# Stick-breaking attention on one Trainium2 core: two passes over V with its high and low parts in one stationary tile, and a bank for each head

## The chip, the cores and the metric

The kernel runs on one core of a Trainium2 chip. A core has five engines with queues of their own: TensorE (matrix products, into the eight PSUM banks of 128 x 512 float32), VectorE, ScalarE, GpSimd, and SyncE, which issues DMAs. Engines work in order, each through its own queue, and meet only at semaphores. The metric is device time in microseconds for one call. `PE`, `PEld`, `DVE`, `ACT`, `POOL` and `SP` in the profile are TensorE's products, TensorE's weight loads, VectorE, ScalarE, GpSimd and SyncE.

## The reference

One sequence of 512 tokens, width 1024, two layers: a stick-breaking attention layer (16 heads of 64), then a differential attention layer on a shared K and V. Only the first layer is touched. Cut to it:

```python
def stick_breaking_attention(q, k, v):          # (B,H,S,D), strictly causal
    z = einsum('bhqd,bhkd->bhqk', q, k) / sqrt(D)
    log_1m = where(strict, log_sigmoid(-z), 0.0)
    suffix = cumsum(log_1m, axis=3, reverse=True) - log_1m
    a = where(strict, exp(log_sigmoid(z) + suffix), 0.0)
    return einsum('bhqk,bhkd->bhqd', a, v)

def stick_breaking_layer(x, norm_g, w_in, w_out):
    h = rms_norm(x, norm_g)
    q, k, v, gate = split(h @ w_in, 4)           # each (S, 1024), heads of 64
    o = stick_breaking_attention(heads(q), heads(k), heads(v))
    return (silu(gate) * o) @ w_out
```

Everything is float32, and the kernel gets float32 accuracy out of products on rounded operands (float32r) by splitting: each operand is a high part (rounded) and a low part (the rest), and a product is hi·hi + hi·lo + lo·hi, three passes of TensorE.

## The kernel before

Each of the five engines has one hand-written program (`@block.tensor`, `@block.vector`, `@block.scalar`, `@block.gpsimd`, `@block.sync`), and what one engine needs of another is a `wait_ge` on a named semaphore. The order inside an engine is therefore the order of the code.

**Stages.** Norm and transpose of the input, the projection of V for all heads (to 78 us of the profile), then eight *pairs* of heads (p = 0 to 7, 128 features each, 78 to 311 us), the first output projection (to about 350 us), then the second layer, which the change does not touch. Pair 0 and pair 7 are written out, pairs 1 to 6 are a loop. Weights come in slabs of 128 x 512 by DMA; GpSimd splits each into `w_hi` (a cast, L468) and `w_lo` (a subtraction, L470).

**A pair on TensorE** (`pair`, L692 to L717). `scores_a(p)` waits for q and k to be split (`s_qk`, L646), puts masks into banks 0 to 5 (L637, L639) and adds the scores (L658), head h in banks 3h to 3h+2. `attend_a(p-1, 1)` then finishes the *previous* pair in bank 7. Then the gate's projection into bank 6, and the projection of the next q into bank 7 in two halves of 12 matmuls of 512 columns, with `suffix_sums(p, 0)` between them; `suffix_sums(p, 1)`; the projection of the next k into bank 6; `attend_a(p, 0)` into bank 7. A projection is 24 matmuls of 512 columns (L560, L561, L562, the lines of `three`). The next pair starts with its scores.

The scores of a head are kept transposed as four causal strips, j = 0 to 3, 512, 384, 256 and 128 columns wide (`STRIP`), 1280 columns in all. `attend_a(p, h)` multiplies each strip of weights (`hi[h]`, `lo[h]`) with the 128 x 128 stationary tile of V for that strip. V lies as `va_hi` and `va_lo`, 192 columns per strip: head 0 at 0 to 63, zeros at 64 to 127, head 1 at 128 to 191. Columns 0 to 127 are thus head 0 beside zeros, columns 64 to 191 zeros beside head 1, and both heads can add into one bank, head 0 in rows 0 to 63 and head 1 in rows 64 to 127:

```python
                v = slice(DH * h, DH * h + P)
                mm = three(o[:, j * P:SEQ], va_hi[:, j, v], va_lo[:, j, v], hi[h][:, seg], lo[h][:, seg],
                           start=(h == 0 and j == 0), stop=(h == 1 and j == TT - 1))
```

**A pair on ScalarE** (L1057 to L1109). For each of the six score banks an abs (`ab`, L1062), an exp (`e`, L1067) and a log (`l`, L1072), interleaved; the gate's copy, abs, exp and log; `weights(h)`: the exponentials of the suffix sums (L1078, L1080); between and after them `q_hi_a` (L1004) and, last in the pair, `k_hi_a` (L1009), the high parts of the next q and k, which wait for their projections.

**A pair on VectorE** (L1374 to L1428). For each score bank `soft` (softplus, L1378, one input in PSUM), `soft_hi` (a cast, L1384) and `soft_lo` (a subtraction, L1389, both inputs in SBUF); `suffix_sums(p, 0)` waits for the three soft_lo of head 0, `suffix_sums(p, 1)` for those of head 1. Behind the first soft_lo stands `gated_a(p-1)` (L1372): the previous pair's output in bank 7 times `silu`. It frees bank 7 (`s_og`, L710) and feeds `keep_hi` and `keep_lo`, the split output that the output projection reads. Then the gate's part, `weights_lo(h)` (L1395), `q_lo_a` (L1324) and, last, `k_lo_a` (L1330).

**GpSimd** splits V for a pair (`values_a`, L482 and L484) once `attend_a(p-1, 1)` is done (`s_pv`), then that pair's slabs.

**Pair 7** has no next q and k. In their place `early_tile` multiplies six kept outputs with the first six slabs of the output weights; `attend_a(7, 1)` runs after the sixth step of the output projection and step k = 7 waits for the last kept output (`s_o`).

## Time and profile before

| | us |
|---|---|
| median of three runs | 695.98 (693.69 to 698.03) |
| the profiled execution, its own time | 692.85 |
| its span, first to last instruction | 691.6 |
| TensorE busy | 646.1 |
| VectorE / ScalarE / GpSimd busy | 433.1 / 328.6 / 343.8 |

The profile is one execution. Its page gives shares of the span; the windows give the same for a stretch, with the clock that TensorE was granted (1.00 is 2.4 GHz, 0.50 is 1.2 GHz); the timeline gives start and length of each instruction, and in brackets how long the engine sat idle before it and what ended that. Matmuls overlap: one's length is longer than the distance to the next, and the distance between two starts is what it costs. The same holds in part for VectorE and ScalarE, whose next instruction can start before the last one's end.

### The profile page before, as it was taken

What the parts mean: (1) busy time and instruction counts of PE and PEld (TensorE: products, weight loads), DVE (VectorE), ACT (ScalarE), POOL (GpSimd) and SP (SyncE); (2) the same over time, 40 slices, a digit from 0 to 9 for tenths busy, and PEclk for the clock granted to TensorE, in tenths of its full rate; (3) what the DMA queues carried; (4) which work ended last, traced back from release to release, by engine and by line L of the source; (5) the groups of instructions that cost most, each with busy time, mean ns of one, the idle gap of its engine ahead of it and who ended that gap; (6) DMA issues with size and microseconds to landing.
All of it is one profiled execution on the core that took longest, in us unless ns stands there. A gap on an engine that the chain in (4) does not pass through costs nothing.

```text
span 691.6 us, 10026 instructions
## 1 busy us (share of the span) xinstructions
PE 646.1 (93%) x3388; PEld 544.9 (79%) x3388; DVE 433.1 (63%) x685; ACT 328.6 (48%) x712; POOL 343.8 (50%) x325
## 2 busy tenths in 40 slices
PE   4999989999999999899989999997899889687998
PEld 4788778888888888788878888886787777576886
DVE  3493295775957758473073788048888899777321
ACT  4342466475664756633255454224564356535220
POOL 5564675544555442445324544485744465253241
PEclk9999999999999999999999999999999999878999
DMA  7432231221212210021112222223222111210141
GB/s 243 119 91 77 67 102 46 62 61 45 61 45 61 61 45 30 16 77 62 65 58 88 95 85 83 84 76 99 78 65 57 34 42 46 87 51 26 50 138 61
DMA packets 61774, 49.08 MB, mean 71 GB/s; under 512 B 7729, under 2 KB 48817, under 8 KB 61745
## 3 DMA queue, kind: packets, MB, share of 16 engines
q1 hardware_dynamic: 58064, 48.25, 22.6%
q10 hardware_dynamic: 3680, 0.46, 0.4%
q8 instruction: 17, 0.28, 0.2%
q14 instruction: 13, 0.10, 0.0%
HBM read 44.50 MB, written 2.10 MB: 67 GB/s over the span
## 4 chain that ended last, share of the span: by engine, by line
PE 72%; DVE 16%; issue 5%; ACT 3%; POOL 2%; DMA 1%; DVEq 0%; SPq 0%; POOLq 0%; ACTq 0%
PE bank L560 19%; PE bank L561 19%; PE bank L562 19%; PE bank L673 6%; DVE small L1585 3%; PE bank L658 2%; DVE ge L1340 1%; DVE pr L1608 1%; PE bank L821 1%; POOL w_lo L470 1%; PE bank L841 1%; DVE v L1308 1%; DVE hi L1384 1%; DMA xs<-in_x 1%; PE bank L637 1%
## 5 line engine op out<-in xcount | busy, mean ns | idle before, releaser
L470 POOL TENSOR_TENSOR w_lo<-w_raw,w_hi 128x512 fp32r<-128x512 f32 x100 | 139.6, 1396 | 8.0
L458 POOL TENSOR_TENSOR w_lo<-w_raw,w_hi 128x512 fp32r<-128x512 f32 x60 | 81.1, 1354 | 122.0 <-ACT w_hi L954 121.6
L468 POOL CAST w_hi<-w_raw 128x512 fp32r<-128x512 f32 x100 | 72.3, 723 | 123.1 <-PE bank L562 74.2
L560 PE MATMUL bank<-h_hi,w_hi 128*128 128x512 f32 x320 | 130.8, 409 | 2.6 <-ACT q L1152 2.6
L560 PE MATMUL bank<-w_hi,h_hi 128*128 128x512 f32 x320 | 127.6, 399 | 4.0 <-DVE h_lo L1314 2.9
L561 PE MATMUL bank<-h_lo,w_hi 128*128 128x512 f32 x320 | 127.1, 397 | 0.0
L562 PE MATMUL bank<-h_hi,w_lo 128*128 128x512 f32 x320 | 126.7, 396 | 0.0
L562 PE MATMUL bank<-w_hi,h_lo 128*128 128x512 f32 x320 | 125.2, 391 | 0.0
L561 PE MATMUL bank<-w_lo,h_hi 128*128 128x512 f32 x320 | 125.1, 391 | 0.0
L560 PEld LDWEIGHTS bank<-h_hi,w_hi 128*128 128x128 f32 x320 | 61.8, 193 | 15.9 <-ACT q L1152 3.0
L954 ACT ACTIVATE w_hi<-w_raw 128x512 fp32r<-128x512 f32 x60 | 37.6, 628 | 77.0 <-PE bank L562 77.0
L560 PEld LDWEIGHTS bank<-w_hi,h_hi 128*128 128x128 f32 x320 | 60.5, 189 | 16.9 <-DVE h_lo L1314 3.5
L562 PEld LDWEIGHTS bank<-h_hi,w_lo 128*128 128x128 f32 x320 | 61.2, 191 | 13.8
L561 PEld LDWEIGHTS bank<-h_lo,w_hi 128*128 128x128 f32 x320 | 61.5, 192 | 11.7
L562 PEld LDWEIGHTS bank<-w_hi,h_lo 128*128 128x128 f32 x320 | 60.2, 188 | 13.2
L561 PEld LDWEIGHTS bank<-w_lo,h_hi 128*128 128x128 f32 x320 | 60.4, 189 | 12.0
L1378 DVE SCALAR_TENSOR_TENSOR sp<-bank,ex 128x512 f32<-128x512 f32 (+1 forms) x48 | 28.4, 593 | 42.8 <-ACT ex L1072 42.8
L1234 ACT ACTIVATE pr<-bank,small 128x512 f32<-128x512 f32 (+3 forms) x64 | 38.8, 616 | 11.8 <-DVE small L1590 11.8
L1389 DVE TENSOR_TENSOR lo<-sp,hi 128x512 fp32r<-128x512 f32 (+1 forms) x48 | 42.6, 888 | 0.6
L1496 DVE TENSOR_TENSOR xs<-bank,xs 128x512 f32<-128x512 f32 x16 | 10.9, 692 | 46.1 <-PE bank L562 46.1
L1395 DVE TENSOR_TENSOR lo<-ex,hi 128x512 fp32r<-128x512 f32 (+1 forms) x48 | 33.5, 752 | 7.4 <-ACT hi L1080 7.4
L1062 ACT ACTIVATE ex<-bank 128x512 f32<-128x512 f32 (+1 forms) x48 | 25.3, 527 | 24.1 <-PE bank L658 23.4
(176 smaller groups left out, 1229.7 us busy)
## 6 DMA issues: line engine op xcount, KB each, us to landing
w_raw<-in_a_w_in SPq DMA_DIRECT2D x64, 256.0 KB, 2.8
w_raw<-in_w_kv SPq DMA_DIRECT2D x32, 256.0 KB, 3.1
w_raw<-in_b_w_in SPq DMA_DIRECT2D x32, 256.0 KB, 2.8
w_raw<-in_a_w_out SPq DMA_DIRECT2D x16, 256.0 KB, 2.7
w_raw<-in_b_w_out SPq DMA_DIRECT2D x16, 256.0 KB, 2.8
xs<-in_x SPq DMA_DIRECT2D x4, 512.0 KB, 5.3
qrot<-qs SPq DMA_DIRECT2D x32, 64.0 KB, 2.0
out_x<-xs SPq DMA_DIRECT2D x8, 256.0 KB, 2.6
```

Of the source, the lines that this page charges most:

```text
L458: nc.gpsimd.tensor_tensor(w_lo[s][:, :], w_raw[s][:, :], w_hi[s][:, :].bitcast(F32), ALU.subtract).then_inc(s_w, 1)
L468: nc.gpsimd.tensor_copy(w_hi[s][:, :], w_raw[s][:, :]).then_inc(s_whi, 1)
L470: nc.gpsimd.tensor_tensor(w_lo[s][:, :], w_raw[s][:, :], w_hi[s][:, :].bitcast(F32), ALU.subtract).then_inc(s_w, 1)
L560: pe.matmul(o, ahi, bhi, start=start, stop=False, skip_group_check=True)
L561: pe.matmul(o, ahi, blo, start=False, stop=False, skip_group_check=True)
L562: return pe.matmul(o, alo, bhi, start=False, stop=stop, skip_group_check=True)
L673: mm = pe.matmul(bank[3 * h + b][:, cols(c, n)], (neg_tri if i == j else neg_one)[:, :], part[h][:, cols(STRIP[i][0], n)], start=False, st ...
L954: A(w_hi[s][:, :], w_raw[s][:, :], ACT.Copy).then_inc(s_whia, 1)
L1234: A(pr[c][:, cols(at, w)], bank[BANK_B[c, b]][:, cols(at - BANKS[b][0], w)], ACT.Exp, bias=tiny[:, 8 + 2 * i + c:9 + 2 * i + c], scale=mea ...
L1378: STT(out=sp[m // 3][:, seg], in0=bank[m][:, 0:BANKS[m % 3][1]], scalar=0.0, op0=ALU.max, in1=ex[m // 3][:, seg], op1=ALU.add).then_inc(s_ ...
L1389: TTN(lo[h][:, seg], sp[h][:, seg], hi[h][:, seg].bitcast(F32), ALU.subtract).then_inc(s_sl, 1)
L1395: TTN(lo[h][:, seg], ex[h][:, seg], hi[h][:, seg].bitcast(F32), ALU.subtract).then_inc(s_al, 1)
```

## The change

V is laid out anew. One tile `va` holds, for each strip and head, 128 stationary columns: the high part of V's 64 columns and its low part side by side, for head 0 high then low, for head 1 low then high. One pass with `hi[h]` and one with `lo[h]` then give, in 64 rows of the bank, the weights times V's high part (rows of that head) and, in the other 64, the weights times V's low part, which contains the lo·lo product too. The two halves must be added, across partitions: ScalarE copies the low half to the head's own rows in SBUF (`correction` into `cor`), VectorE adds (`sum_output` into `osum`), and `gated_a` takes `osum` in place of the bank. Since a head now fills a whole bank, head 0 goes into bank 0 (free once its weights are made) and head 1 into bank 7 (bank 3 in pair 7). `attend_a(p, 0)` moves from behind the key projection to between its halves, and the wait for q_lo ahead of it goes. The scores wait for head 0's sum (bank 0), the projection of q waits for head 1's (bank 7). On ScalarE head 1's correction stands between `l(1)` and `ab(3)` of the next pair, head 0's behind `weights(1)`; on VectorE head 1's sum takes the place that `gated_a` had, which moves behind `soft_hi(1)`, and head 0's stands behind `weights_lo(1)`. GpSimd splits V with four instructions per pair in place of two, and the two memsets of the old tiles go. In pair 7 head 1's correction stands behind the slab G_OUT + 11 on ScalarE.

```diff
--- before.py
+++ after.py
@@ -198,8 +198,9 @@
     w_raw += [sb(f"w_raw{i}", [P, 512], F32, phase_a) for i in (4, 5)]
     w_hi += [sb(f"w_hi{i}", [P, 512], F32R, phase_a) for i in (4, 5)]
     w_lo += [sb(f"w_lo{i}", [P, 512], F32R, phase_a) for i in (4, 5)]
-    va_hi = sb("va_hi", [P, TT, 192], F32R, phase_a)
-    va_lo = sb("va_lo", [P, TT, 192], F32R, phase_a)
+    va = sb("va", [P, TT, 2, P], F32R, phase_a)
+    cor = sb("cor", [P, SEQ], F32, phase_a)
+    osum = sb("osum", [P, SEQ], F32, phase_a)
     ex = [sb(f"ex{h}", [P, CAUSAL], F32, phase_a) for h in (0, 1)]
     sp = [sb(f"sp{h}", [P, CAUSAL], F32, phase_a) for h in (0, 1)]
     hi = [sb(f"hi{h}", [P, CAUSAL], F32R, phase_a) for h in (0, 1)]
@@ -268,6 +269,9 @@
     s_al = sem("weights_split")
     s_v = sem("v_split")
     s_pv = sem("block_output_ready")
+    s_pa = sem("first_output_ready")
+    s_cor = sem("correction_copied")
+    s_os = sem("output_summed")
     s_gc = sem("gate_copied")
     s_ga = sem("gate_abs")
     s_gx = sem("gate_exp")
@@ -313,7 +317,7 @@
     wout_b = b_w_out.rearrange("o (k p) n -> p (o k) n", p=P)
     x_rows = x.rearrange("o (t p) n -> p (o t) n", p=P)
     out_rows = out.rearrange("o (t p) n -> p (o t) n", p=P)
-    va_parts = [v[:, :, :].rearrange("p j (a b) -> p j a b", a=3)[:, :, 0:3:2, :] for v in (va_hi, va_lo)]
+    va_parts = [[va[:, :, h, cols(DH * (h ^ part), DH)] for h in (0, 1)] for part in (0, 1)]
     ang = ex[0][:, 0:640]
     turns, absr = ex[1][:, 0:640], sp[1][:, 640:1280]
     sines = sp[0]
@@ -440,11 +444,10 @@
         nc.gpsimd.affine_select(out=g32[:, 2 * P:3 * P], in_=big, compare_op=ALU.is_gt, fill=0.0, base=0,
                                 pattern=[[1, P]], channel_multiplier=-1)
         nc.gpsimd.memset(ones_c, 1.0)
-        nc.gpsimd.memset(va_hi[:, :, :].bitcast(F32), 0.0)
         st.link(nc.gpsimd.memset(sel, 0.0))
         st.link(nc.gpsimd.memset(sel[0:DH, 0:1], 1.0))
-        st.link(nc.gpsimd.memset(sel[DH:P, 1:2], 1.0))
-        nc.gpsimd.memset(va_lo[:, :, :].bitcast(F32), 0.0).then_inc(s_cst, 1)
+        nc.gpsimd.memset(sel[DH:P, 1:2], 1.0).then_inc(s_cst, 1)
+        pool.wait_ge(s_cst, 1)
 
         def waited():
 
@@ -472,9 +475,19 @@
 
         def values_a(p):
 
-            src = v32[:, :, bass.ds(p * P, P)].rearrange("p j (a b) -> p j a b", a=2)
             pool.wait_ge(s_pv, p)
-            split_v(src, va_parts[0], va_parts[1])
+            split_pair([v32[:, :, bass.ds(p * P + DH * h, DH)] for h in (0, 1)])
+
+        def split_pair(src):
+
+            waited()
+            for h in (0, 1):
+                ins = nc.gpsimd.tensor_copy(va_parts[0][h], src[h])
+            st.link(ins)
+            waited()
+            for h in (0, 1):
+                ins = nc.gpsimd.tensor_tensor(va_parts[1][h], src[h], va_parts[0][h].bitcast(F32), ALU.subtract)
+            ins.then_inc(s_v, 1)
 
         def split_v(src, dhi, dlo):
 
@@ -488,7 +501,7 @@
         pool.wait_ge(s_vk, V_BY_ACT)
         pool.wait_ge(s_vkd, 2)
 
-        split_v(v32[:, :, 0:P].rearrange("p j (a b) -> p j a b", a=2), va_parts[0], va_parts[1])
+        split_pair([v32[:, :, cols(DH * h, DH)] for h in (0, 1)])
         for g in range(G_BODY + 2, G_BODY + 12):
             split(g)
         with pool.Fori(1, KT - 2) as i:
@@ -646,6 +659,7 @@
             pe.wait_ge(s_qk, p * 2 + 2)
             if not first:
                 pe.wait_ge(s_ah, p * 6)
+                pe.wait_ge(s_os, p * 2 - 1)
             for h in (0, 1):
                 for b in range(3):
                     mask(bank[3 * h + b][:, :], 0, len(BANK_STRIPS[b]), 3 * P, mask_a)
@@ -675,19 +689,19 @@
                                            skip_group_check=True)
                 mm.then_inc(s_t, 1)
 
-        def attend_a(p, h, o=bank[7]):
+        def attend_a(p, h, o=None):
 
 
             if h == 0:
                 pe.wait_ge(s_v, p + 1)
             pe.wait_ge(s_al, p * 6 + (3 * h + 3))
+            o = o or bank[7 if h else 0]
             for j in range(TT):
-                v = slice(DH * h, DH * h + P)
                 seg = cols(*STRIP[j])
-                mm = three(o[:, j * P:SEQ], va_hi[:, j, v], va_lo[:, j, v], hi[h][:, seg], lo[h][:, seg],
-                           start=(h == 0 and j == 0), stop=(h == 1 and j == TT - 1))
-            if h == 1:
-                mm.then_inc(s_pv, 1)
+                for w in (hi, lo):
+                    mm = pe.matmul(o[:, j * P:SEQ], va[:, j, h, :], w[h][:, seg], start=(j == 0 and w is hi),
+                                   stop=(j == TT - 1 and w is lo), skip_group_check=True)
+            mm.then_inc(s_pv if h else s_pa, 1)
 
         def pair(p, first=False, last=False):
 
@@ -698,23 +712,21 @@
             project(G_GLAST if last else G_BODY, h1_hi, h1_lo, bank[6][:, :], p, 0 if last else 6)
             if last:
                 suffix_sums(p, 0)
-                pe.wait_ge(s_og, p)
+                pe.wait_ge(s_os, p * 2)
                 early_tile(0)
                 pe.wait_ge(s_gc, p + 1)
                 pe.wait_ge(s_ga, p + 1)
                 early_tile(1)
                 suffix_sums(p, 1)
-                attend_a(p, 0, bank[0])
+                attend_a(p, 0)
                 return
             if not first:
-                pe.wait_ge(s_og, p)
+                pe.wait_ge(s_os, p * 2)
             project(G_BODY + 2, h1_hi, h1_lo, bank[7][:, :], p, 6, between=lambda: suffix_sums(p, 0))
             suffix_sums(p, 1)
             pe.wait_ge(s_gc, p + 1)
             pe.wait_ge(s_ga, p + 1)
-            project(G_BODY + 4, h1_hi, h1_lo, bank[6][:, :], p, 6)
-            pe.wait_ge(s_qk, p * 2 + 3)
-            attend_a(p, 0)
+            project(G_BODY + 4, h1_hi, h1_lo, bank[6][:, :], p, 6, between=lambda: attend_a(p, 0))
 
         def early_tile(t):
 
@@ -734,7 +746,7 @@
         pair(KT - 1, last=True)
         for k in range(EARLY):
             bulk_step(G_OUT + k, 0, k, h2_hi, h2_lo, banks_of=OUT_BANK_A, tiles=(2, 3))
-        attend_a(KT - 1, 1, bank[0])
+        attend_a(KT - 1, 1, bank[3])
         for k in range(EARLY, KT):
             pe.wait_ge(s_o, k + 1)
             bulk_step(G_OUT + k, 0, k, h2_hi, h2_lo, banks_of=OUT_BANK_A)
@@ -1087,6 +1099,8 @@
             l(0)
             e(2)
             l(1)
+            if not first:
+                correction(p - 1, 1, bank[7])
             ab(3)
             l(2)
             ab(4)
@@ -1105,8 +1119,17 @@
             if not last:
                 q_hi_a(p * 6 + (G_BODY + 4))
             weights(1)
+            correction(p, 0, bank[0], first)
             if not last:
                 k_hi_a(p * 6 + (G_BODY + 6))
+
+        def correction(p, h, o, first=False):
+
+            act.wait_ge(s_pv if h else s_pa, p + 1)
+            if not first:
+                act.wait_ge(s_os, p * 2 + (h - 1))
+            main, other = slice(DH * h, DH * h + DH), slice(DH - DH * h, P - DH * h)
+            A(cor[main, :], o[other, :], ACT.Copy).then_inc(s_cor, 1)
 
         pair(0, first=True)
         with act.Fori(1, KT - 1) as i:
@@ -1114,7 +1137,10 @@
         pair(KT - 1, last=True)
 
 
-        for g in range(G_OUT + RING_A, G_OUT + 14):
+        for g in range(G_OUT + RING_A, G_OUT + 12):
+            slab_hi(g)
+        correction(KT - 1, 1, bank[3])
+        for g in range(G_OUT + 12, G_OUT + 14):
             slab_hi(g)
         for t in range(TT):
             squares(1, t, 0)
@@ -1366,10 +1392,16 @@
             keep_hi(p, n)
             keep_lo(p, n)
 
-        def gated_a(p, o=bank[7]):
-
-            dve.wait_ge(s_pv, p + 1)
-            TTN(og[:, :], o[:, :], silu[:, :], ALU.mult).then_inc(s_og, 1)
+        def sum_output(p, h, o):
+
+            main = slice(DH * h, DH * h + DH)
+            dve.wait_ge(s_cor, p * 2 + (h + 1))
+            TTN(osum[main, :], o[main, :], cor[main, :], ALU.add).then_inc(s_os, 1)
+
+        def gated_a(p):
+
+            dve.wait_ge(s_os, p * 2 + 2)
+            TTN(og[:, :], osum[:, :], silu[:, :], ALU.mult).then_inc(s_og, 1)
 
         def pair(p, first=False, last=False):
             def soft(m):
@@ -1399,8 +1431,10 @@
             soft(1)
             soft_lo(0)
             if not first:
+                sum_output(p - 1, 1, bank[7])
+            soft_hi(1)
+            if not first:
                 gated_a(p - 1)
-            soft_hi(1)
             soft(2)
             soft_lo(1)
             soft_hi(2)
@@ -1424,6 +1458,7 @@
             if not last:
                 q_lo_a(p * 2 + 3)
             weights_lo(1)
+            sum_output(p, 0, bank[0])
             if not last:
                 k_lo_a(p * 2 + 4)
 
@@ -1485,7 +1520,8 @@
             pair(i)
             st.leave(KT - 2)
         pair(KT - 1, last=True)
-        gated_a(KT - 1, bank[0])
+        sum_output(KT - 1, 1, bank[3])
+        gated_a(KT - 1)
         keep_output(KT - 1, KT)
 
         def add_residual(g, m, half, banks_of=range(8)):
```

## Rows read from the trace of the kernel before

**Rows 1.** The page, busy time of each engine (share of the span), instructions
```profile
PE 646.1 (93%) x3388; PEld 544.9 (79%) x3388; DVE 433.1 (63%) x685; ACT 328.6 (48%) x712; POOL 343.8 (50%) x325
```

**Rows 2.** Windows: length, busy us (instructions) per engine, PEclk (granted clock), DMA, GB/s
```profile
166.00:195.00 29.00, 29.00 (x170) 25.19 (x169) 20.35 (x31) 17.63 (x37) 14.87 (x15) 1.00 0.19 54
...
199.60:212.95 13.35, 13.35 (x67) 11.29 (x67) 13.20 (x22) 10.13 (x22) 8.07 (x8) 1.00 0.20 59
```

**Rows 3.** Timeline of TensorE, a hand-over: start, length (start us, us), line, form, count
```profile
192.72 0.39 PE L560 MATMUL bank<-hi,va_hi 128*128 128x512 f32 x1
...
194.57 0.28 PE L637 MATMUL bank<-mask_a,ident_r 128*128 128x128 f32 x1
...
197.46 0.50 PE L560 MATMUL bank<-hi,va_hi 128*128 128x512 f32 x1
...
199.43 0.45 PE L560 MATMUL bank<-h_hi,w_hi 128*128 128x512 f32 x1
...
223.40 0.28 PE L637 MATMUL bank<-mask_a,ident_r 128*128 128x128 f32 x1
```

**Rows 4.** Timeline of TensorE, the suffix sums of the same pair
```profile
207.81 0.40 PE L673 MATMUL bank<-hi,neg_tri 128*128 128x512 f32 x1
...
209.03 0.39 PE L673 MATMUL bank<-hi,neg_tri 128*128 128x384 f32 x1
...
213.31 0.40 PE L673 MATMUL bank<-hi,neg_tri 128*128 128x512 f32 x1
```

**Rows 5.** Timelines of ScalarE (first row) and VectorE in the same pair
```profile
192.91 0.60 ACT L1009 ACTIVATE k_hi<-bank 128x512 fp32r<-128x512 f32 x1 [3.84 <-PE bank L562]
...
193.55 0.69 DVE L1330 TENSOR_TENSOR k_lo<-bank,k_hi 128x512 fp32r<-128x512 f32 x1 [2.83 <-ACT k_hi L1009]
...
201.28 1.22 DVE L1389 TENSOR_TENSOR lo<-sp,hi 128x512 fp32r<-128x512 f32 x1
...
203.43 0.41 DVE L1378 SCALAR_TENSOR_TENSOR sp<-bank,ex 128x256 f32<-128x256 f32 x1
...
208.01 0.68 DVE L1378 SCALAR_TENSOR_TENSOR sp<-bank,ex 128x512 f32<-128x512 f32 x1
...
208.61 0.69 DVE L1389 TENSOR_TENSOR lo<-sp,hi 128x512 fp32r<-128x512 f32 x1
...
212.50 0.43 DVE L1389 TENSOR_TENSOR lo<-sp,hi 128x256 fp32r<-128x256 f32 x1
```

**Rows 6.** Timelines of ScalarE and GpSimd in the same pair
```profile
200.77 0.42 ACT L1072 ACTIVATE ex<-ex 128x256 f32<-128x256 f32 x1
...
200.66 1.29 POOL L484 TENSOR_TENSOR va_lo<-v,va_hi 128x512 fp32r<-128x512 f32 x1 [0.19 <-POOL va_hi L482]
```

**Rows 7.** VectorE's groups, shapes apart, six looped pairs: busy us, mean ns, idle before
```profile
L1389 DVE TENSOR_TENSOR lo<-sp,hi 128x512 fp32r<-128x512 f32 x24 | 24.2, 1007 | 0.0
...
L1372 DVE TENSOR_TENSOR og<-bank,silu 128x512 f32<-128x512 f32 x6 | 4.1, 678 | 0.0
```

**Rows 8.** Timelines of TensorE and VectorE, pair 7 and the output projection
```profile
302.92 0.50 PE L560 MATMUL bank<-w_hi,h_hi 128*128 128x512 f32 x1 [1.05 <-POOL w_lo L470]
...
324.07 0.69 DVE L1362 TENSOR_TENSOR h_lo<-og,h_hi 128x512 fp32r<-128x512 f32 x1
...
325.47 0.39 PE L560 MATMUL bank<-w_hi,h_hi 128*128 128x512 f32 x1
```

**Rows 9.** Windows of pair 7, columns as in the second group
```profile
291.70:293.78 2.08, 0.05 (x1) 0.00 (x0) 2.05 (x3) 1.93 (x4) 2.00 (x3) 1.00 0.34 126
...
295.44:298.85 3.41, 3.41 (x15) 3.22 (x14) 3.41 (x5) 2.08 (x5) 3.25 (x5) 0.50 0.27 95
```

**Rows 10.** Timelines of TensorE in pair 0 and of GpSimd at the start
```profile
97.88 0.50 PE L673 MATMUL bank<-hi,neg_tri 128*128 128x512 f32 x1 [1.34 <-DVE lo L1389]
...
2.79 0.74 POOL L443 MEMSET va_hi<- 128x768 f32 x1
```

## The prediction

> **What bounds the kernel now.** I read the page's engine shares first: TensorE is busy 93% of the span [rows 1]. An average does not say what a change in one stage is worth, so next I took the windows of the stick-breaking stage: in a stretch as long as one looped head pair TensorE is busy for 29.00 of 29.00 us at the full clock, GpSimd for half of it [rows 2]. The masks of two pairs start at 194.57 and 223.40, so a pair takes 28.83 us [rows 3]. In this stage matmul time is the time, as long as nothing that TensorE waits for comes later. The last view, the timelines of one pair, tells how far each such thing is from coming later, and that decides this change.
>
> Three slacks matter. (1) After the key projection, k_hi (ScalarE) and k_lo (VectorE) must be made before the next pair's scores. The first slot after the projection is at 192.72; k_lo ends at 193.55 + 0.69 = 194.24; the masks start at 194.57 [rows 3, 5]. The wait is hidden by `attend_a(p, 0)`, which fills 192.72 to 194.57. (2) `suffix_sums(p, 1)` starts at 213.31 and needs the last soft_lo, which ends at 212.50 + 0.43 = 212.93: 0.38 us of room, or 0.34 after the 0.04 that a release takes (k_hi ends at 192.91 + 0.60 = 193.51, k_lo starts at 193.55) [rows 4, 5]. (3) From 199.60 to 212.95 VectorE is busy for 13.20 of 13.35 us [rows 2]: what is added there moves its end.
>
> **The change, part by part.**
>
> *The third pass goes.* Each head has 4 strips x 3 matmuls, 1.85 us (192.72 to 194.57) for head 0 and 1.97 (197.46 to 199.43) for head 1 [rows 3]. After it, 4 strips x 2. The first eight matmuls of the suffix sums have just these widths, two each of 512, 384, 256 and 128: 207.81 to 209.03 = 1.22 us [rows 4]. That is 0.63 less per head, 16 x 0.63 = 10.1 us of matmul time in all.
>
> *Head 0 moves between the halves of the key projection.* It keeps its cost, now 1.22, but no longer covers the copies of k: those end at 194.24, released 0.04 later, against the slot at 192.72, a wait of 1.56 us. From projection to masks it was 1.85; now it is 1.22 + 1.56 = 2.78. That is +0.93 at seven hand-overs (pair 0 to 1, up to 6 to 7): **+6.5 us**.
>
> *ScalarE's correction of head 0 and VectorE's sum* stand ahead of k_hi and k_lo in their queues. A matmul of 512 takes 0.233 (199.43 to 207.81 is 36 of them [rows 3, 4]), so head 0 ends 12 x 0.233 = 2.8 us ahead of the projection's end; correction (as k_hi, 0.60) and sum (as k_lo, 0.69) are over more than 1 us before it. No cost; without that cover k_hi would be late by what is missing. The scores' new wait on this sum costs nothing either: k_lo comes later in the same queue.
>
> *Head 1's correction on ScalarE, ahead of `ab(3)`.* Head 1 starts at 197.46 and now ends near 198.8. `l(2)` runs at 200.77, one slot behind `ab(3)` [rows 6], so ScalarE comes to the correction near 200.3, does not wait, and loses about 0.5 us. Queued behind it are l(2) and head 1's softplus. l(2) then ends near 201.7, and soft(2), which needs it, starts at 203.43 [rows 5]; those behind have more. Hidden.
>
> *VectorE's front.* `sum_output(p-1, 1)` is one more instruction on PSUM, 0.60 us of queue time (208.01 to 208.61 [rows 5]). Beside it `gated_a` changes kind: its input was a bank, now both inputs are in SBUF. The bank form took 678 ns in the loop; soft_lo of the same size with both inputs in SBUF took 1007 on average [rows 7], though 0.69 at best. At 201.28 it took 1.22 and ended soon after a GpSimd instruction did (200.66 + 1.29 = 201.95) [rows 5, 6]. So I add 0.33 and get e = 0.93. Lower bound 0.60 (the gating meets no GpSimd work), upper 0.60 + 1.3 = 1.9 (it waits for a whole GpSimd subtraction). In this stretch GpSimd is busy 8.07 of 13.35 us, so meeting it is likelier than not. TensorE comes 0.63 earlier, VectorE 0.93 later, 0.34 is room: a wait of 1.2 us, and suffix_sums(p, 1) starts 0.59 later after the scores than before. Pair 0 has neither sum nor gating ahead of it and pair 7 waits elsewhere, so six pairs: **+3.5 us**, between the bounds +1.6 and +9.4. Head 1's own 0.63 is swallowed here.
>
> That the two-input form waits behind GpSimd is what these rows show. The Trainium skill (SBUF — State Buffer, "Who interferes with whom") has it as a rule: a VectorE instruction with two SBUF inputs contends with a GpSimd instruction that reads SBUF, and one with at most one, outside the two-port modes, does not. By that rule the gating leaves the safe kind; had it stayed, this term would be 6 x 0.26 = 1.6 us.
>
> *Pair 7 and the end.* GpSimd splits v after head 1 of pair 6, then six slabs, and TensorE waits for the sixth until 302.92 [rows 8]. The splitting starts 0.63 earlier, but does four instructions instead of two; and half an instruction costs more than half its time: 0.19 us pass even between the two now [rows 6], I estimate 0.15 for each of the two added, 0.3 in all: -0.3. A later VectorE chain is covered by this wait. Head 0: -0.63. Head 1: -0.63, but output step k = 7 needs the gated output, there at 324.07 + 0.69 = 324.76 against its slot at 325.47, room 0.71 [rows 8]. Correction and sum put 0.60 + 0.69 + 0.08 = 1.37 into that chain: +0.66. Net 0. Together **-0.9 us**.
>
> *GpSimd's split of v in the loop*: four instructions of half the size on an engine busy half the time. Nothing. *The start*: two memsets of 0.74 leave [rows 10] and the warm-up matmuls start 1.5 us earlier; the first products wait for DMA, ScalarE and VectorE. I take 0. TensorE's idle time before the transposes grows by as much; should the clock rise later for it, that could cost what one stretch at the lower clock costs (B below), 1.7.
>
> **Sum.** 6.5 + 3.5 - 0.9 = 9.1 us, slower. The profiled execution took 692.85 (span 691.6); the median of the runs, 695.98, is 3.1 above it, and waits add alike to both: 702.0 beside the profile's time, **705.1** beside the median.
>
> **Rivals.**
>
> *A: VectorE absorbs its extra work.* For it: in the loop the 24 wide soft_lo alone lose 24 x 0.32 = 7.6 us behind GpSimd, 1.3 per pair [rows 7], and GpSimd's work now starts 0.63 earlier after the scores, so these losses may shrink. Against it: the sum is certain, the shrinking is luck. With e at -0.29 or lower TensorE sets the pace, -0.63 per pair: 6.5 - 3.8 - 0.9 = +1.8, **697.8**, not slower than can be told. It decides from e = 0.57 down, where the sum falls below 7.0.
>
> *B: the clock falls after the new waits.* After some 2.03 us of idling up to 293.78 the granted clock was 0.50 from 295.44 to 298.85: 3.41 us at 1.2 instead of 2.4 GHz, 1.7 lost. After 1.34 us of idling before 97.88 it stayed at 1.00 [rows 9, 10]. The new waits, 1.6 and 1.2, lie between or below. If four of the seven hand-overs met it: +6.8, **711.9**.
>
> *C: the lock at its upper bound.* e = 1.9: 6.5 + 9.4 - 0.9 = 15.0, **711.0**.
>
> *D: no wait is exposed and the change brings its matmul time*: -10.1, **685.9**. Against it stands the order: nothing is left between the key projection and the scores, whose first instruction waits for k_lo. It needs the two copies of k to take nearly no time.
>
> **How the numbers follow.** Forecast (e from 0.57 to 1.5, no fall of the clock) 0.52; A 0.22; B 0.09; C 0.11; D 0.06. The likeliest gives 705.1; its own range is 703 to 709. The range reaches from A's 697.8 to B's 711.9, rounded outwards, and leaves out D and the far sides of B and C, under 2 in 10. One per cent is 7 us, about what a measurement of this kernel can tell from no change. Slower: B, C and all of the forecast but 0.06 that other mis-sized terms bring under 702.9: 0.66. Same: A and that 0.06: 0.28. Faster: D, 0.06.
>
> **What would show it.** Right: 64 matmuls fewer; a head's attention near 1.22 us; TensorE idle about 1.6 us before each of seven first masks, released by k_lo, and about 1.2 before suffix_sums(p, 1), released by soft_lo; a pair every 28.83 + 0.93 + 0.59 = 30.35 us; the gating above 0.68 in some pairs. Wrong: a pair in under 29.9 us (A), a granted clock of 0.50 inside the loop (B), a wait for a correction or a sum before the last pair, or masks that start without a wait (D).

## The result, and the profile after

The changed kernel takes 709.19 us (median of six runs, 706.75 to 709.92) against 697.53 for the kernel before on the same chip: ratio **1.017**, 95% interval 1.014 to 1.020, some 12 us slower. Forecast was 9.1 us slower, 705.1 in the range 697.5 to 712.5. The profiled execution took 708.09 us, 15.2 more than that of before. The medians differ by 11.7: the execution profiled before took 4.7 us less than the median of its kernel's six runs, this one 1.1 less, so 3.6 of the 15.2 are not the change's. The page after, against [rows 1]:

```profile
PE 643.1 (91%) x3324; PEld 535.8 (76%) x3324; DVE 451.3 (64%) x701; ACT 337.1 (48%) x728; POOL 347.5 (49%) x339
```

TensorE has 64 matmuls less, yet its busy time is only 3.0 us less; the 15.2 us and these 3 are idle time. The removed matmuls are 10.1 us at their pace. What makes up for most of them is that two stretches ran at the lower clock which the kernel before does not have (below, about 1.7 us each), and that at each new wait the last matmul's length, 0.39 where the next slot is 0.23 on, counts as busy and the first one behind the wait is slow. The masks of the eight pairs tell where it lies. All in us, the first matmul of each:

| | before | after | difference |
|---|---|---|---|
| start to first masks of pair 0 | 78.71 | 79.62 | +0.9 |
| first masks to suffix_sums(p, 1), pair 0 | 19.17 | 19.46 | +0.3 |
| the same, pairs 1 to 6, sum | 112.48 | 118.37 | +5.9 |
| suffix_sums(p, 1) to the next masks, seven, sum | 70.70 | 79.47 | +8.8 |
| pair 7 and output projection, to the start of its last addition | 69.28 | 69.39 | +0.1 |
| second layer | 341.2 | 340.5 | -0.7 |

**The hand-over.** Timeline of TensorE after, answering to [rows 3]: head 0 between the halves of the key projection, the projection's last matmul, the masks.

```profile
197.68 0.39 PE L702 MATMUL bank<-hi,va 128*128 128x512 f32 x1
...
198.90 0.45 PE L573 MATMUL bank<-h_hi,w_hi 128*128 128x512 f32 x1
...
201.48 0.39 PE L575 MATMUL bank<-h_hi,w_lo 128*128 128x512 f32 x1
203.45 0.32 PE L650 MATMUL bank<-mask_a,ident_r 128*128 128x128 f32 x1 [1.59 <-DVE k_lo L1356]
```

And ScalarE (first two rows) and VectorE beside it, against [rows 5]:

```profile
199.18 0.60 ACT L1132 ACTIVATE cor<-bank 64x512 f32<-64x512 f32 x1 [2.43 <-PE bank L702]
201.90 0.60 ACT L1021 ACTIVATE k_hi<-bank 128x512 fp32r<-128x512 f32 x1 [2.12 <-PE bank L575]
...
199.81 0.68 DVE L1399 TENSOR_TENSOR osum<-bank,cor 64x512 f32<-64x512 f32 x1 [0.78 <-ACT cor L1132]
202.53 0.69 DVE L1356 TENSOR_TENSOR k_lo<-bank,k_hi 128x512 fp32r<-128x512 f32 x1 [2.04 <-ACT k_hi L1021]
```

Head 0 takes 198.90 - 197.68 = 1.22 us, as forecast. Then the last matmul of the key projection starts at 201.48, the next slot would be 201.71, the masks start at 203.45, released by k_lo. Correction and sum are over (199.81 + 0.68 = 200.49) when k_hi starts: they do not hold it up. The waits of TensorE for one line each, total, number, longest, over the pairs:

```profile
PE bank L650 <- DVE k_lo L1356: 11.0, 7, 1.6
PE bank L687 <- DVE lo L1421: 5.7, 10, 1.1
```

Seven waits for k_lo, and ten for soft_lo. **The front.** The two waits for soft_lo in a pair, against [rows 4], and VectorE in the next pair, against [rows 5]:

```profile
185.87 0.50 PE L687 MATMUL bank<-hi,neg_tri 128*128 128x512 f32 x1 [0.64 <-DVE lo L1421]
...
192.06 0.50 PE L687 MATMUL bank<-hi,neg_tri 128*128 128x512 f32 x1 [0.41 <-DVE lo L1421]
```

```profile
208.56 0.69 DVE L1410 SCALAR_TENSOR_TENSOR sp<-bank,ex 128x512 f32<-128x512 f32 x1 [5.34 <-ACT ex L1084]
...
211.33 0.69 DVE L1399 TENSOR_TENSOR osum<-bank,cor 64x512 f32<-64x512 f32 x1
212.06 1.38 DVE L1416 CAST hi<-sp 128x512 fp32r<-128x512 f32 x1
213.36 0.68 DVE L1404 TENSOR_TENSOR og<-osum,silu 128x512 f32<-128x512 f32 x1
...
215.01 1.38 DVE L1416 CAST hi<-sp 128x256 fp32r<-128x256 f32 x1
...
222.62 0.42 DVE L1421 TENSOR_TENSOR lo<-sp,hi 128x256 fp32r<-128x256 f32 x1
```

GpSimd in the same stretch:

```profile
211.85 1.30 POOL L473 TENSOR_TENSOR w_lo<-w_raw,w_hi 128x512 fp32r<-128x512 f32 x1
...
214.59 1.65 POOL L473 TENSOR_TENSOR w_lo<-w_raw,w_hi 128x512 fp32r<-128x512 f32 x1
```

Two casts (soft_hi, L1416) take 1.38 us: that at 212.06 ends at 213.44, behind GpSimd's instruction of 211.85 + 1.30 = 213.15; that at 215.01 at 216.39, behind 214.59 + 1.65 = 216.24. VectorE's groups in the six looped pairs, before, beside [rows 7], and after:

```profile
L1384 DVE CAST hi<-sp 128x512 fp32r<-128x512 f32 x24 | 18.3, 762 | 0.4
...
L1389 DVE TENSOR_TENSOR lo<-sp,hi 128x256 fp32r<-128x256 f32 x12 | 7.7, 641 | 0.4
...
L1384 DVE CAST hi<-sp 128x256 fp32r<-128x256 f32 x12 | 3.4, 281 | 0.0
```

```profile
L1416 DVE CAST hi<-sp 128x512 fp32r<-128x512 f32 x24 | 21.8, 909 | 0.6
...
L1421 DVE TENSOR_TENSOR lo<-sp,hi 128x512 fp32r<-128x512 f32 x24 | 16.9, 703 | 0.0
...
L1416 DVE CAST hi<-sp 128x256 fp32r<-128x256 f32 x12 | 10.0, 834 | 0.0
...
L1421 DVE TENSOR_TENSOR lo<-sp,hi 128x256 fp32r<-128x256 f32 x12 | 5.6, 463 | 0.4
L1404 DVE TENSOR_TENSOR og<-osum,silu 128x512 f32<-128x512 f32 x6 | 5.2, 863 | 0.0
```

The cast of 512 columns has gone from 762 to 909 ns, that of 256 from 281 to 834, while soft_lo has gone from 1007 to 703 and from 641 to 463. The waits have moved to other instructions; their total has hardly changed (the four groups take 54.3 us for 53.6). The gating's mean of 863 ns hides that it took 0.68 us in five of the six pairs, as before, and this once in the sixth:

```profile
244.50 1.78 DVE L1404 TENSOR_TENSOR og<-osum,silu 128x512 f32<-128x512 f32 x1
```

**The clock.** Windows of the hand-over into pair 5 and of the stretch behind it:

```profile
232.90:234.50 1.60, 0.02 (x1) 0.00 (x0) 0.69 (x1) 0.60 (x1) 1.32 (x2) 1.00 0.44 131
236.34:239.75 3.41, 3.41 (x22) 2.99 (x19) 0.00 (x0) 2.68 (x6) 0.00 (x0) 0.50 0.26 75
```

Here, after 1.59 us of idling, the granted clock fell to 0.50. Behind the six other hand-overs, which idle for 1.41 to 1.64 us, it stayed at 1.00. The pair took 32.32 us where the three ahead of it took 31.04 to 31.08. At the start, from 21.3 to 24.7 us, it was 0.50 too, and in the kernel before it was not; the stretch in pair 7, from 311.6 on, the kernel before has as well [rows 9].

### The profile page after: what moved, and what is told of

Its sections match the earlier page's. It is cut to its first block, busy times and chain, and to the rows that moved or that the text cites. A ratio compares the mean times of both kernels' runs of the same rounds, so it can differ in the third digit from the quotient of the medians.

```text
span 706.8 us, 9976 instructions
## 1 busy us (share of the span) xinstructions
PE 643.1 (91%) x3324; PEld 535.8 (76%) x3324; DVE 451.3 (64%) x701; ACT 337.1 (48%) x728; POOL 347.5 (49%) x339
## 4 chain that ended last, share of the span: by engine, by line
PE 57%; DVE 26%; issue 9%; ACT 6%; DMA 1%; DVEq 0%; SPq 0%; ACTq 0%
PE bank L573 14%; PE bank L575 14%; PE bank L574 14%; PE bank L687 5%; DVE lo L1421 3%; DVE hi L1416 3%; DVE small L1621 3%; DVE sp L1410 2%; PE bank L672 2%; DVE pr L1644 2%; ACT ex L1079 2%; PE bank L702 2%; DVE ge L1366 1%; PE bank L833 1%; PE bank L650 1%
## 5 line engine op out<-in xcount | busy, mean ns | idle before, releaser
L1416 DVE CAST hi<-sp 128x512 fp32r<-128x512 f32 (+1 forms) x48 | 44.5, 928 | 0.8
```

What stands on the lines that cost most here:

```text
L1416: V.tensor_copy(hi[m // 3][:, seg], sp[m // 3][:, seg]).then_inc(s_sh, 1)
```

## The experiments

Each ran beside the kernel before on the same chip; ratios are to that kernel, with their 95% intervals. "Period" is the distance between the first masks of two looped pairs, "front" that from the first masks to suffix_sums(p, 1).

### The move alone

```diff
-            project(G_BODY + 4, h1_hi, h1_lo, bank[6][:, :], p, 6)
-            pe.wait_ge(s_qk, p * 2 + 3)
-            attend_a(p, 0)
+            project(G_BODY + 4, ..., between=lambda: head0(p))   # head0: the same wait and attend_a(p, 0)
```

> The kernel before with one part of the change alone: attend_a(p, 0), still three passes, moved between the halves of the key projection. My theory (the move takes away what covered the copies of k): each of seven hand-overs gains a wait of 1.74 us, the size seen in the profile after, and 0.1 for the restart, so about +12.9 us, the loop's period 30.7 us, TensorE idle about 1.6 us before each of seven first masks. Rival (the changed kernel is slower because of its added instructions, not because of the move): between 0 and +2 us, since no instruction is added.

Measured 707.17 us, ratio 1.017 (1.014 to 1.021), +12.4 us. Period 30.60, front 18.79 (18.75 before). TensorE ahead of one of the masks:

```profile
171.42 0.32 PE L637 MATMUL bank<-mask_a,ident_r 128*128 128x128 f32 x1 [1.49 <-DVE k_lo L1333]
```

One moved call, no added instruction, costs as much as the whole change. The rival falls. In the changed kernel the hand-overs cost 8.8 us, less than here, where they cost 7 x 1.7, because head 0 is 0.63 us shorter there. Here the masks start 0.13 to 0.14 us behind k_lo's end in the loop, in the changed kernel 0.23 to 0.28.

### The third pass alone, with nothing in its place

```diff
-                mm = three(o[:, j * P:SEQ], va_hi[:, j, v], va_lo[:, j, v], hi[h][:, seg], lo[h][:, seg], ...)
+                for w in (hi, lo):
+                    mm = pe.matmul(o[:, j * P:SEQ], va_hi[:, j, v], w[h][:, seg], ...)
```

> The kernel before without its third pass and with nothing in its place: the product of V's low part is left out, so this computes less. It tells what 64 matmuls fewer are worth at best in the old order. Theory 1 (matmul time is the time): 16 x 0.63 = -10.1 us. Theory 2 (mine, by the slacks): head 0's 1.22 us no longer cover the 1.75 us of the copies of k, so a hand-over gains 0.1 and not 0.63; the front gains at most the 0.34 us that VectorE leaves; pair 7 and the end give about -1.9: 7 x -0.1 - 6 x 0.34 - 1.9 = -4.6 us, with new idle time of about 0.4 us before each first mask and about 0.3 before suffix_sums(p, 1).

Measured 694.36 us, ratio 1.000 (0.998 to 1.002). Both theories fall: in this order 64 matmuls fewer are worth nothing. In five looped pairs the period is 29.42 us, *longer* than 28.83, the front 19.42 for 18.75 (pair 6, beside which GpSimd has less to do, takes 28.66). TensorE's waits in the loop, and VectorE's softplus groups in the same window as [rows 7]:

```profile
PE bank L673 <- DVE lo L1390: 4.6, 11, 0.4
```

```profile
L1385 DVE CAST hi<-sp 128x512 fp32r<-128x512 f32 x24 | 23.4, 973 | 0.4
L1390 DVE TENSOR_TENSOR lo<-sp,hi 128x512 fp32r<-128x512 f32 x24 | 20.8, 867 | 0.0
L1385 DVE CAST hi<-sp 128x256 fp32r<-128x256 f32 x12 | 10.0, 832 | 0.0
L1390 DVE TENSOR_TENSOR lo<-sp,hi 128x256 fp32r<-128x256 f32 x12 | 5.1, 425 | 0.4
```

The four groups take 59.3 us here, 53.6 before. No instruction of VectorE or GpSimd was changed, only the moment at which TensorE finishes with a slab, and with it the moment at which GpSimd starts on the next. The casts take 11.7 us more than before, soft_lo 6.0 less. So the front of the kernel before was as quick as it was because GpSimd's instructions happened to fall where they cost VectorE less; 0.6 us earlier, they fall on its casts. In pair 7 some time is gained, 1.2 us, although about 6.8 us ran at a granted clock of 0.50 there, twice what the kernel before meets, which costs up to 1.7 us of the gain. The same kernel once more, to exclude that it is one execution's chance:

> A second look at the kernel before without its third pass (the product of V's low part is left out). Theory: the loop's period is 29.4 us again, longer than with the third pass, with two waits of about 0.4 us for soft_lo, since it is not chance but the order of GpSimd's and VectorE's instructions. Rival (one execution's chance): a period between 28.2 and 28.8.

Measured: period 29.40 to 29.44 in the same five pairs, front 19.41 to 19.43, the two waits again, casts 975 and 831 ns, 695.35 us in its one run beside a median of 693.84. Not chance.

### A shorter front for VectorE

In the changed kernel, `gated_a(p - 1)`, `keep_hi(p - 1, p)` and `keep_lo(p - 1, p)` are taken out of the softplus front and stand behind `gate_log(p + 1)`.

> The changed kernel with gated_a, keep_hi and keep_lo of the pair before moved on VectorE from the softplus front to behind gate_log; the sum of head 1 stays in the front. Theory (VectorE's front sets the start of the suffix sums): 1.65 us leave a front that is late by 1.06 in all, TensorE sets the pace again, the start of suffix_sums(p, 1) after the first mask goes from 19.65 to about 18.2 us, the period from 31.05 to 29.6, in all about -9 us against the changed kernel (700). Rival (ScalarE's correction ahead of ab(3) or GpSimd's four instructions hold the front): no more than -2.

Measured 704.88 us, ratio 1.015 (1.011 to 1.020). The front went from 19.65 to between 18.81 and 18.88, the period from 31.05 to between 29.92 and 30.17, in the pairs at the full clock; two pairs met the lower clock (30.96 and 31.68 us), which in the changed kernel's profile one had. TensorE's waits:

```profile
PE bank L650 <- DVE k_lo L1356: 9.4, 6, 1.6
PE bank L687 <- DVE lo L1421: 2.1, 5, 0.4
```

The direction of the theory holds, its size does not: of 1.65 us taken out of VectorE's queue 0.8 arrive, and a wait of 0.43 before suffix_sums(p, 0) is left of 0.65. In total the run cannot be told from the changed kernel's ratio.

### Head 0 back behind the key projection

```diff
-            project(G_BODY + 4, ..., between=lambda: attend_a(p, 0))
+            project(G_BODY + 4, ...)
+            pe.wait_ge(s_qk, p * 2 + 3)
+            attend_a(p, 0, bank[7])
```

`correction(p, 0)` and `sum_output(p, 0)` follow k_hi and k_lo, and `attend_a(p - 1, 1)` waits for that sum.

> The changed kernel with head 0 back behind the key projection, in bank 7, and its correction and sum behind k_hi and k_lo; head 1 waits for that sum. Theory (the copies of k are the hand-over's cost): the wait before the first mask falls from 1.59 us to about 0.4, a hand-over costs 1.3 us less, 7 x -1.3 = -9 us against the changed kernel (700), period 29.7 us. Rival (a head that fills a bank needs a wait somewhere: head 1's new wait for the sum takes its place): less than -3, with TensorE idle before attend_a(p-1, 1), released by the sum.

Measured 698.93 us, ratio 1.007 (1.004 to 1.010), by the ratios 1.0% or 7 us less than the changed kernel. Period 29.44 to 29.66 in pairs 1 to 5, front 19.54 to 19.64, as in the changed kernel. The waits:

```profile
PE bank L686 <- DVE lo L1423: 5.9, 10, 1.1
PE bank L650 <- DVE k_lo L1358: 1.6, 6, 0.3
```

The wait before the masks is 0.3 instead of 1.6, and none stands before head 1: the rival falls. What is left to the kernel before is the front.

### GpSimd's split of V later

In the loop `values_a` moves from ahead of the six slabs to behind the fourth, in pair 7 behind the six slabs of the output weights; once in the kernel before, once in the changed kernel.

> The kernel before with GpSimd's split of V moved, in each looped pair, from ahead of the slabs to behind the fourth slab, and in pair 7 behind the six slabs of the output weights. Theory (TensorE alone sets the loop's pace in the kernel before, VectorE's waits behind GpSimd are hidden there): period 28.8 us as it was; the gain is only in pair 7, whose slabs come earlier (idle 2.03 and 1.05 us there): -2 to -3 us. Rival (VectorE's waits do not come from GpSimd's instructions): the softplus instructions soft_hi and soft_lo of 128x512, 762 and 1007 ns on average in the loop, stay as long.

Measured 688.69 us, ratio 0.992 (0.989 to 0.994), -5.8 us. The period is 28.83 in all six pairs. From pair 7's masks to the start of the output projection's last addition it took 64.8 us for 69.3: the idle 2.03 is 0.49, the wait of 1.05 for the sixth slab is gone, and the granted clock, which fell to 0.50 there before, stays at 1.00, which is another 1.7. The rival about the instructions holds in part: soft_hi of 512 is now at 964, soft_lo at 700, and the four softplus groups take 55.0 us for 53.6. With the split of V moved away the waits did not become fewer, they only changed place, so most of them lie behind the slabs' instructions.

> The changed kernel with GpSimd's split of V moved behind the fourth slab (in pair 7 behind the six). Theory (the front is late because VectorE waits behind GpSimd): the waits for soft_lo, 0.65 and 0.41 us per pair, go, the period falls from 31.05 to about 30.0, pair 7 loses most of its 4.63 us of idling: -9 us against the changed kernel (700). Rival (VectorE's added sum and gating alone make the front late): the front stays within 0.3 us of 19.65, only pair 7 gains, -2 to -3.

Measured 709.36 us, ratio 1.021 (1.016 to 1.026). The theory falls, and the front stays within 0.3 us of 19.65, as the rival had it. In four pairs it is 19.40 to 19.42 and the period 31.2, and pair 7 with the output projection takes 68.1 us for 69.4; the two other pairs met the lower clock (32.1 and 31.9). The waits for soft_lo and a new one, for V itself:

```profile
PE bank L690 <- DVE lo L1424: 3.3, 8, 0.4
PE bank L705 <- POOL va L489: 2.5, 6, 0.9
```

### All three moves

> The changed kernel with all three moves: head 0 behind the key projection in bank 7, gating and keeping out of VectorE's front, GpSimd's split of V behind the fourth slab. Theory: TensorE sets the pace again with two passes, the period is 28.83 - 0.63 - 0.1 = 28.1 us or a little over, pair 7 gains 2 to 3 us as the kernel before would: about -8 us against the kernel before (688). Rival (two passes cannot pay in this order, since whatever TensorE gains in the front brings GpSimd's slabs, and with them VectorE's waits, forward): a period of 28.8 or more, 693 to 697.

Measured 707.37 us, ratio 1.017 (1.012 to 1.022). The front is right at last (18.58 in pair 1, with no wait of note for soft_lo), but k_lo comes late. VectorE, TensorE, and the window that follows:

```profile
166.82 4.07 DVE L1432 TENSOR_TENSOR lo<-ex,hi 128x512 fp32r<-128x512 f32 x3
170.81 0.68 DVE L1361 TENSOR_TENSOR k_lo<-bank,k_hi 128x512 fp32r<-128x512 f32 x1
...
171.62 0.47 PE L653 MATMUL bank<-mask_a,ident_r 128*128 128x128 f32 x1 [2.48 <-DVE k_lo L1361]
...
171.62:178.40 6.78, 6.78 (x34) 5.95 (x35) 0.47 (x1) 2.72 (x6) 0.00 (x0) 0.50 0.13 39
```

`weights_lo(1)`, three instructions, takes 4.07 us where it takes 2.03 in the changed kernel's loop and 1.63 in pair 0. The last two slabs, which GpSimd now splits behind V, lie beside it, and TensorE idles 2.48 us. After each of the six waits (2.38 to 2.48 us) the granted clock fell to 0.50, for up to 6.8 us, and periods behind them were 31.7 to 33.3. This is the forecast's rival B, in a kernel that was not the forecast's.

### soft_hi computed from the bank

```diff
-                V.tensor_copy(hi[m // 3][:, seg], sp[m // 3][:, seg])
+                STT(out=hi[m // 3][:, seg], in0=bank[m][:, 0:BANKS[m % 3][1]], scalar=0.0, op0=ALU.max,
+                    in1=ex[m // 3][:, seg], op1=ALU.add)
```

> The changed kernel with one kind of instruction exchanged: soft_hi is no longer a cast of sp (SBUF to SBUF) but the softplus computed once more from the bank, rounded on writing (one input in PSUM, one in SBUF). Uncontended it is longer by 0.27 us (512 columns) and 0.13 (256). Theory (the front is late because VectorE's SBUF-only instructions wait for whole GpSimd instructions): the casts lose 3.4 us per pair to those waits now, so in spite of the longer form the front is over 1 us or more sooner, the waits for soft_lo (0.65 and 0.41) go, period 31.05 to about 29.9, pair 7 gains 2: about -8 us against the changed kernel (701). Rival (VectorE's front is late by the number and length of its instructions): +1.26 us per pair, period 32.3, +7 us (716).

Measured 705.70 us, ratio 1.015 (1.009 to 1.021). Both fall in the loop: a period of 31.2 in four pairs and 29.42 in one (30.8 in the sixth, at the lower clock for a stretch). The new form never waits, but gating and keeping now do:

```profile
L1415 DVE SCALAR_TENSOR_TENSOR hi<-bank,ex 128x512 fp32r<-128x512 f32 x24 | 16.4, 681 | 0.2
...
L1404 DVE TENSOR_TENSOR og<-osum,silu 128x512 f32<-128x512 f32 x6 | 7.0, 1162 | 0.0
...
L1382 DVE CAST h_hi<-og 128x512 f32 x6 | 5.9, 980 | 0.0
```

The gating took 1.03 or 1.04 us in five pairs and 1.80 in one. In the pair of 29.42 us the front took 18.13, TensorE's own time; in the four others 19.83, with a wait of 1.11 before suffix_sums(p, 1). The gating of the kernel before, one input in PSUM, took 678 ns. In pair 0, which has no gating and no keeping in its front and where VectorE sets the pace, the exchange gave what was hoped: 28.15 for 30.89.

### What these point to

The next takes, on top of the changed kernel, head 0 behind the key projection, the shorter front, and the later split of V in pair 7 alone:

> The changed kernel with head 0 behind the key projection in bank 7, gating and keeping out of VectorE's front, and, in pair 7 alone, GpSimd's split of V behind the six slabs. Theory: the hand-over as in the run with head 0 behind the projection, the front as in the run with the shorter front: period 29.65 - 0.77 = 28.9 us, that of the kernel before, and pair 7's gain of 5 us: 689, equal to the kernel before with the same edit in pair 7, so two passes bring nothing. Rival (k_lo comes late, as in the run with all moves in the loop, because gating and keeping now stand ahead of it): period over 30, with idle time above 0.5 us before the first mask.

Measured 692.97 us, ratio 0.999 (0.996 to 1.001). Period 29.04 for the 28.9 expected, wait before the masks 0.57: the rival's mechanism is there, small. The total is 4 us over the expectation, three of them in pair 7 and the output projection, which take 67.8 us where the kernel before with the later split of V took 64.8. They have an idle 2.84 us there for 0.49, and the granted clock falls to 0.50 behind it, which costs 1.7. Then the same with soft_hi from the bank:

> The same as the last one, and soft_hi computed from the bank instead of cast. Theory: with the casts out of GpSimd's way TensorE sets the pace in the front, and only the copies of k are left: period 28.83 - 0.63 - 0.1 = 28.1 to 28.3 us, 6 x -0.6 = -4 us against the last one (685). Rival (soft_lo takes over the waits that the casts had): the front no sooner, period 28.8 to 29.

Measured **680.43 us, ratio 0.979** (0.973 to 0.985), faster than both. Period 28.03, front 18.13, and this is all that TensorE waits for in the loop, followed by soft_lo's group:

```profile
PE bank L651 <- DVE k_lo L1359: 1.6, 6, 0.3
```

```profile
L1425 DVE TENSOR_TENSOR lo<-sp,hi 128x512 fp32r<-128x512 f32 x24 | 21.8, 909 | 0.0
```

soft_lo did take over some waits (909 ns), but with gating and keeping out of the front and the casts out of GpSimd's way they no longer reach TensorE. Pair 0 takes 26.75 us. Two of these edits have nothing to do with the change, so the kernel before gets them too:

> The kernel before (three passes, both heads in bank 7) with the two edits that do not belong to the change: soft_hi from the bank, and GpSimd's split of V in pair 7 behind the six slabs. It is what the two passes have to beat. Theory (each edit only takes away a wait that is exposed): the loop stays at 28.83 us, TensorE's own time; pair 0 gains 2.7 us as in the two runs with soft_hi from the bank, pair 7 about 5: 686 us, so that of the 13.5 us by which the last kernel beat the kernel before, two passes account for 5 to 6. Rival (the gain of the last kernel is that of soft_hi and pair 7 alone): 681 or less.

Measured 689.15 us, ratio 0.991 (0.987 to 0.994). Loop 28.83, pair 0 27.43 for 29.36, pair 7 and the output projection 65.4 for 69.3. The rival falls: the last two kernels differ by 8.7 us, or 1.2% by their ratios to the kernel before. Of these the profiles show 4.9 in the loop (0.8 per pair), 0.7 in pair 0 and 1.0 in pair 7; the rest lies in stages where the two kernels do the same. Some 6.6 us are thus what two passes are worth with the waits out of the way, of 10.1 us of matmuls. The two kernels also differ in where gating and keeping stand, and the kernel before with that edit as well was not run; in its loop no wait is left that it could take away.

## Why the prediction was right

The median is 4.1 us above the forecast's 705.1. Of this 1.5 is the kernel before, whose median rose from 695.98 to 697.53 with three more runs; the change cost 11.7 where 9.1 was forecast. By the stages of the two profiles it cost 15.2, 3.6 of which are those executions' own, so the terms below add up to more than the medians show. The places and the order of size were right, and the terms missed in the same direction, so the total is not right because errors cancelled; inside the term of the front they did.

**The third pass, 0.63 us per head: right.** There are 64 matmuls fewer and head 0 takes 1.22 us.

**The hand-over, +6.5: right in mechanism, short in size, +8.8.** It was priced at 0.93 and costs 1.3 in most pairs. The wait after the projection's last slot is 1.74, not 1.56: k_lo ends at 203.22 and the first mask starts 0.23 later, where I took 0.04, a release between ScalarE and VectorE, for one into TensorE. Of these 0.23 some 0.10 go with a term that I put at nothing, the scores' new wait on head 0's sum. In the loop the masks start 0.23 to 0.28 us behind k_lo's end in the four kernels that have this wait ahead of them, and 0.13 to 0.15 in the six whose masks wait for k_lo too but not for the sum. Ahead of pair 7, outside the loop, it is 0.05 to 0.06 in all ten. What in the waits takes the time is not shown. The other 0.19 is what TensorE needs to come back into step: the first matmul after a wait or behind the 128-column ones lies 0.29 to 0.34 before the next, not 0.23, and there are more such places. That the move is the cause is shown by the kernel with the move alone and by the one with the move undone.

**Correction and sum of head 0, head 1's correction on ScalarE, GpSimd's four instructions: no cost, right but for the 0.10 above.** No wait of TensorE names them. GpSimd needs 2.56 us for its split of V where it needed 2.09, 0.47 more and not 0.3.

**VectorE's front, +3.5: the place right, the mechanism half.** The front is late by 5.9 us in six pairs, of which 1.3 is the lower clock in one, so 4.6. In the pair whose masks start at 203.45 the last soft_lo ends 222.62 + 0.42 - 203.45 = 19.59 us behind them, before it was 212.93 - 194.57 = 18.36. So e is 1.23, not 0.93, and less the room of 0.34 this gives 0.89: the front of this pair is 0.91 longer. But e is not made as I made it. The sum holds the queue for 0.73 (211.33 to 212.06), not 0.60. The gating, for which I added 0.33, met no GpSimd work in five pairs of six and added nothing. The front's casts are 1.96 us longer in this pair and its soft_lo 1.77 shorter, the front starts 0.07 later, and the rest is small gaps. That 0.93 came this near is in part luck. I had let the rest of the queue keep its waits. Here their sum nearly stayed, though they sit on other instructions. The kernel without a third pass shows that it need not: with nothing added, the front is 0.67 later only because TensorE is earlier. I had counted TensorE's 0.63 as swallowed; it does harm. Rival A had the same coupling and guessed its sign as a gain. The row that could have warned me was there: soft_lo at 1007 against 0.69 uncontended is 1.3 us per pair of waits whose place depends on when slabs come free.

The rule named in the prediction (the Trainium skill, SBUF — State Buffer, "Who interferes with whom") agrees with the gating as far as that goes: with one input in SBUF it took 678 ns on average, with two 0.68 us in five pairs of the changed kernel and 1.78 in one, and 1162 ns on average where the casts no longer wait in its stead. Whether it waits depends on where GpSimd stands. The same section says that casts can take the port pair that VectorE shares with GpSimd, and that whoever starts first holds it for the whole instruction. The two casts of 1.38 us that end just behind GpSimd's instructions agree. I weighed the rule for the one instruction that changed kind and not for those around it.

**Pair 7 and the end, -0.9: wrong by 1.0, it is +0.1.** The step that failed is "a later VectorE chain is covered by this wait":

```profile
311.62 0.80 PE L687 MATMUL bank<-hi,neg_tri 128*128 128x512 f32 x1 [4.63 <-DVE lo L1421]
...
305.41 1.38 DVE L1416 CAST hi<-sp 128x512 fp32r<-128x512 f32 x1
306.71 1.09 DVE L1404 TENSOR_TENSOR og<-osum,silu 128x512 f32<-128x512 f32 x1
...
310.12 1.44 DVE L1421 TENSOR_TENSOR lo<-sp,hi 128x256 fp32r<-128x256 f32 x1
```

And the same cast in the kernel before:

```profile
289.50 0.41 DVE L1384 CAST hi<-sp 128x512 fp32r<-128x512 f32 x1
```

TensorE idles 4.63 us there for 2.03. The second cast took 1.38 for 0.41, the sum added 0.73, the gating took 1.09 for 0.68; the narrow soft_lo took 1.44 for 1.45, so it is not to blame. The chain is 2.0 us later behind the masks, a little over the upper bound of e (1.9), and outlasts the wait for the slab, which no longer shows. The end itself came as worked out: an idle 0.53 us before step k = 7, forecast 0.66.

```profile
341.30 0.50 PE L573 MATMUL bank<-w_hi,h_hi 128*128 128x512 f32 x1 [0.53 <-DVE h_lo L1388]
```

**The start, 0: +0.9 in the profile.** TensorE's idle time before the transposes grew to 3.69 us, and from 21.3 to 24.7 the granted clock was 0.50, which it was not before. Of the eight kernels without the two memsets five show such a stretch near 21 us, of the six with them one (the move alone). That is a hint and no proof, and it was not tried by itself. The 0.9 us are not tied to it either: the first masks start between 78.57 and 80.36 us in the six kernels with the memsets, between 79.43 and 80.59 in the eight without.

Wrong in the forecast's list of signs: I expected one wait of 1.2 us before suffix_sums(p, 1); there are two, 0.65 before suffix_sums(p, 0) and 0.41 before suffix_sums(p, 1). A pair takes 31.05 us, not 30.35. And B's sign, a granted clock of 0.50 inside the loop, came once in seven hand-overs.

## What to carry to other kernels

Before work is taken from the engine that is always busy, list what it covers: here 0.63 us per head was less than the 1.56 us of two copies that head 0 hid, and undoing the move gave 7 us, as much as the removed matmuls gave at best (6.6). Where VectorE and GpSimd both work out of SBUF, a change in a third engine's pace moves their collisions; so first take the collisions out (a cast replaced by a second computation from PSUM, longer by 0.27 us and never blocked in these runs), then shorten. An edit that gives nothing alone can be what makes another pay: by the ratios, the shorter front and the form from PSUM brought 0.2% each to the changed kernel, which cannot be told from nothing, the hand-over 1.0%, and all together with pair 7's edit 3.8%.

## What the runs showed of the hardware that I had not expected

Without a third pass, 64 matmuls fewer, the loop's period grew from 28.83 to 29.42 us, twice. The release by VectorE of TensorE's first mask took 0.23 us (k_lo's end at 203.22 to 203.45), 0.13 in the loop of the kernels with one wait fewer ahead of it, and 0.06 outside the loop. The granted clock can fall after an idle time of 1.4 to 1.6 us: once in the seven hand-overs of the changed kernel, twice each with the shorter front, with the later split of V and with soft_hi from the bank, and not once with the move alone (1.41 to 1.50 us of idling). It fell after each of 2.38 to 2.48; what separates the shorter cases is open.
